# Tile 0's value rows summed by VectorE; other tiles' slots in fours, with one Gelu and one product for their diagonals; convolution taps spread over 40 positions

## What is computed

```python
z = x @ w_in                                  # q, k, v (8 heads x 64), GLU value and gate
att = dilated sliding-window attention        # prompt: over 1024 keys; sample: over a cache
conv = swish(LN(causal depthwise conv, 31 taps))
x1 = LN(ALPHA * x + concat(att, conv) @ w_out)
# PEER: 8 heads; each takes the 16 best of 128 x 128 product keys -> 128 experts a token
act = gelu(einsum('td,tkd->tk', x1, expert_u[e]))      # k = 128 slots
coef = softmax(best scores) * act
y = LN(ALPHA * x1 + einsum('tk,tkd->td', coef, expert_v[e]))
```

## Time and profile before

| | |
|---|---|
| median of 3 runs | 4052.86 us (4046.16 to 4052.99) |
| the profiled execution: its time | 4054.08 us |
| its span | 4052.3 us |
| DMA traffic over the span | 1385.80 MB, 342 GB/s |
| tile 0, first dot to tile 1's first dot | 909.6 us |
| tiles 1 to 6, from first dot to first dot | 2266.1 us together |
| tile 7 / tile 8 and the end | 505.1 us / 172.0 us |

### The profile page before, as it was taken

How to read it: one execution, slowest core, us unless ns; L and a number is a source line. 1 busy time by engine, 2 the same in 40 slices (tenths; PEclk the granted TensorE clock), 3 DMA queues, 4 the chain that set the end, 5 groups by cost and what they waited for, 6 DMA issues and landing times.

```text
span 4052.3 us, 41343 instructions
## 1 busy us (share of the span) xinstructions
PE 2865.7 (71%) x14768; PEld 1255.5 (31%) x14768; DVE 2703.9 (67%) x7412; ACT 682.6 (17%) x1484; POOL 1203.4 (30%) x1092
## 2 busy tenths in 40 slices
PE   6976554778567667666766876687677666779766
PEld 5422221334222313332332333233223332223311
DVE  4233343335586998699679868976997696445965
ACT  1200012210022013102310330132014101121000
POOL 0011111111144433433444344424333442223232
PEclk8987777889788888888888888879878988889989
DMA  9954468577689998998999899979988999999888
GB/s 334 345 202 155 151 225 290 206 277 291 226 328 408 411 366 326 422 413 345 372 419 400 330 395 419 394 290 416 414 355 325 421 408 391 415 417 365 335 329 349
DMA packets 217518, 1385.80 MB, mean 342 GB/s; under 512 B 27416, under 2 KB 38168, under 8 KB 66648
## 3 DMA queue, kind: packets, MB, share of 16 engines
q0 software_dynamic: 156672, 1140.92, 70.6%
q1 hardware_dynamic: 40384, 142.88, 9.8%
q10 hardware_dynamic: 20256, 99.35, 6.4%
HBM read 1369.94 MB, written 80.04 MB: 358 GB/s over the span
## 4 chain that ended last, share of the span: by engine, by line
PE 33%; DMA 29%; DVE 25%; issue 10%; POOL 2%; ACT 1%; DVEq 0%; ACTq 0%; POOLq 0%; SPq 0%
DMA t<-in_expert_uv,t 28%; PE psum L1367 20%; DVE t L1036 8%; PE psum L1214 4%; DVE t L1047 3%; PE psum L1256 2%; PE psum L1234 2%; POOL t L603 2%; DVE t L984 1%; DVE t L982 1%; DVE t L985 1%; DVE t L983 1%; PE psum L1245 1%; DVE t L927 1%; DVE t L981 1%
## 5 line engine op out<-in xcount | busy, mean ns | idle before, releaser
L1367 PE MATMUL psum<-t,t 64*64 64x512 f32 x5696 | 1627.2, 712 | 777.9 <-DVE t L1047 777.6
L603 POOL DMA_INDIRECT t<-in_expert_uv,t x1088 | 1203.2, 1106 | 2819.4 <-PE psum L1367 1403.2
L1036 DVE CUSTOM_DVE_ANT_0 t<-t,t 128x1024 f32<-128x1024 f32 x1088 | 1325.2, 1222 | 1039.0 <-DMA t<-in_expert_uv,t 1031.5
L1367 PEld LDWEIGHTS psum<-t,t 64*64 64x64 f32 x5696 | 415.9, 155 | 1746.1 <-DVE t L1047 983.1
L1363 PE MATMUL psum<-t,t 64*64 64x512 f32 x2496 | 760.4, 738 | 0.0
L754 ACT ACTIVATE t<-t 128x2 f32<-128x2 f32 x544 | 110.6, 203 | 2472.5 <-DVE t L1036 2465.6
L1047 DVE TENSOR_SCALAR t<-t,t,t 128x64 f32<-128x64 f32 x1088 | 294.0, 321 | 68.0 <-ACT t L754 59.1
L1324 PEld LDWEIGHTS psum<-t,t 128*128 128x128 f32 x2304 | 271.7, 197 | 54.0 <-issue 53.9
L1324 PE MATMUL psum<-t,t 128*128 128x128 f32 (+1 forms) x2304 | 281.8, 282 | 0.0
L1214 PE MATMUL psum<-t,t 128*128 128x128 f32 (+2 forms) x768 | 253.8, 489 | 8.2 <-DMA t<-in_xT 7.5
L903 DVE SCALAR_TENSOR_TENSOR t<-t,t,t 128x128 f32<-128x128 f32 x840 | 237.8, 344 | 0.0
(11 more groups left out here) (132 smaller groups left out, 1965.4 us busy)
## 6 DMA issues: line engine op xcount, KB each, us to landing
t<-in_wq_t ACTq DMA_DIRECT2D x63, 1024.0 KB
out<-in_cache_k_win SPq DMA_DIRECT2D x8, 4080.0 KB
out<-in_cache_v_win SPq DMA_DIRECT2D x8, 4080.0 KB
t<-in_w_in_t ACTq DMA_DIRECT2D x44, 512.0 KB, 5.1
t<-in_kc_t SPq DMA_DIRECT2D x8, 2560.0 KB
t<-in_vc_t SPq DMA_DIRECT2D x8, 2560.0 KB, 13.7
t<-in_expert_uv,t POOLq DMA_INDIRECT x1088
t<-in_w_v_t ACTq DMA_DIRECT2D x6, 1024.0 KB, 8.6
```

Of the source, the lines that this page charges most:

```text
L603: pool.indirect_dma_start(ring[:, r, :], None, I["expert_uv"], bass.IndirectOffsetOnAxis(ap=idn[t % 2][:, s:s + 1], axis=0)).then_inc(land ...
L1036: dve.tensor_tensor_reduce(out=ring[:, r, 0:D], in0=x1[t % 2][:, :], in1=ring[:, r, 0:D], scale=1.0, scalar=0.0, op0=ALU.mult, op1=ALU.add ...
L1367: last = pe.matmul(MAIN[t][half][NS * a:NS * a + NS, :], zt[NS * a:NS * a + NS, k % Z_RING, j, :], vv[NS * a:NS * a + NS, :], start=(p == ...
```

## The change

Tile 0's slots no longer go to TensorE. VectorE multiplies a pair's two Gelus with their gates and then adds each slot's v half, scaled by the token's weight, to a sum of 128x1024 in PSUM (`first_values`); it raises `v_done` slot by slot, and `gather` of the slot four later waits for that. In the other tiles four slots make a batch: one Gelu of 128x4, on VectorE one product of 128x4 with the gates and one product of 128x4x64 for the four diagonals, on TensorE the four slots' products one after the other and one step of `pv`. `zt` has two buffers of four. VectorE handles a batch one position after its last slot, behind that position's `dot`; TensorE at the same position. In stage -1 there are 48 slots of tile 0 (49 before), so that their gates are those of three heads. The taps are spread over 40 positions. The steps between attention and routing move: conv LayerNorm to g 10 to 12, both halves of the output projection to g 13 (i = 1 and 3), the LayerNorm of `x1` to g 14 and 15, `queries` and `query_copy` from i = 1 and 2 to i = 3 of their group. The diff, cut to its core:

```diff
 RING, FIRST_RING = 9, 4
-Z_RING = 3
-PAIRS = SLOTS // 2
+Z_RING = 2
+PAIRS, QUADS = SLOTS // 2, SLOTS // 4
...
+TAP_SPAN = 40
...
-EARLY = ROUTE_STEP
-EARLY_GATES = (EARLY * (PH - 1) + TOP - 1) // TOP
+EARLY = 3 * TOP
+EARLY_GATES = EARLY // TOP
...
-AUX_PAIRS = range(8, PAIRS - 4)
+AUX_QUADS = range(3, QUADS - 2)
...
-    early = EARLY * (PH - 1)
     if n < 0:
-        lo, hi = (min(max(q + j - ROUTE_AT - ROUTE_STEP, 0), early) for j in range(2))
+        lo, hi = (min(max(q + j - ROUTE_AT - ROUTE_STEP, 0), EARLY) for j in range(2))
     elif n == 0:
-        lo, hi = (early + (q + j) * (SLOTS - early) // SLOTS for j in range(2))
+        lo, hi = (EARLY + (q + j) * (SLOTS - EARLY) // SLOTS for j in range(2))
...
+def batch(t):
+    return 4 if t else 2
...
+def tap_at(q):
+    return range(q * CK // TAP_SPAN, (q + 1) * CK // TAP_SPAN) if q < TAP_SPAN else range(0)
...
-        zt = small([P, Z_RING, 2, NS])
+        zt = small([P, Z_RING, 4, NS])
...
                 r, use = spot(t, s)
                 if t == 0:
                     if s >= FIRST_RING:
-                        pool.wait_ge(pv, pair(0, s - FIRST_RING) + 1)
+                        pool.wait_ge(v_done, s - FIRST_RING + 1)
                 else:
                     k = (t - 1) * SLOTS + s
                     if k >= RING:
-                        pool.wait_ge(pv, pair(1, k - RING) + 1)
+                        pool.wait_ge(pv, (k - RING) // 4 + 1)
                     elif k < FIRST_RING:
-                        pool.wait_ge(pv, pair(0, SLOTS - FIRST_RING + k) + 1)
+                        pool.wait_ge(v_done, SLOTS - FIRST_RING + k + 1)
                     elif k == FIRST_RING:
...
-            def gelu(t, p):
-                act.wait_ge(a_dot, SLOTS * t + 2 * p + 2)
-                d_ = dots[t % 2][:, 2 * p:2 * p + 2]
+            def gelu(t, c):
+                w = batch(t)
+                act.wait_ge(a_dot, SLOTS * t + w * (c + 1))
+                d_ = dots[t % 2][:, w * c:w * (c + 1)]
                 act.activation(d_, d_, ACT.Gelu).then_inc(a_gelu, 1)
...
-                act.wait_ge(pv, PAIRS * t + AUX_PAIRS.stop)
+                act.wait_ge(pv, quad(t, AUX_QUADS.stop))
...
+                for h in range(PH):
+                    if g == QUERY_AT[h] and i == 3:
+                        query_copy(m, h)
+                        if h == 0:
+                            x1_rows(m)
                 if i != 2:
                     return
-                if g == 9:
+                if g == 11:
                     conv_std(m)
-                if g == 10:
+                if g == 12:
                     conv_swish(m)
                     attended(m)
                     route_loads(m)
-                if g == 13:
+                if g == 14:
                     ln1_std(m)
-                if g == 14:
...
                         score_copy(m, h)
-                    if g == QUERY_AT[h]:
-                        query_copy(m, h)
-                        if h == 0:
-                            x1_rows(m)
...
                                          scalar=0.0, op0=ALU.mult, op1=ALU.add, accum_out=dots[t % 2][:, s:s + 1]).then_inc(a_dot, 1)
-            def weigh(t, p):
-                k = PAIRS * t + p
-                dve.wait_ge(a_gelu, k + 1)
+            def weigh(t, c):
+                k = quad(t, c)
+                d4, g4 = dots[t % 2][:, 4 * c:4 * c + 4], gtn[t % 2][:, 4 * c:4 * c + 4]
+                dve.wait_ge(a_gelu, gelus(t, c) + 1)
+                step(dve.tensor_tensor(d4, d4, g4, ALU.mult))
                 if k >= Z_RING:
                     dve.wait_ge(pv, k - Z_RING + 1)
-                for j in range(2):
-                    s = 2 * p + j
-                    dve.tensor_scalar(zt[:, k % Z_RING, j, :], ident2[:, :], dots[t % 2][:, s:s + 1], gtn[t % 2][:, s:s + 1],
-                                      ALU.mult, ALU.mult).then_inc(zt_ready, 1)
+                dve.tensor_tensor(zt[:, k % Z_RING, :, :], ident2[:, :].unsqueeze(1).broadcast_to([P, 4, NS]),
+                                  d4.unsqueeze(2).broadcast_to([P, 4, NS]), ALU.mult).then_inc(zt_ready, 1)
+            def first_values(c):
+                d2 = dots[0][:, 2 * c:2 * c + 2]
+                dve.wait_ge(a_gelu, gelus(0, c) + 1)
+                step(dve.tensor_tensor(d2, d2, gtn[0][:, 2 * c:2 * c + 2], ALU.mult))
+                for s in (2 * c, 2 * c + 1):
+                    r, _ = spot(0, s)
+                    w_ = dots[0][:, s:s + 1]
+                    if s == 0:
+                        dve.tensor_scalar(first_sum, ring[:, r, D:ROW], w_, None, ALU.mult).then_inc(v_done, 1)
+                    else:
+                        dve.wait_ge(v_done, s)
+                        dve.scalar_tensor_tensor(first_sum, ring[:, r, D:ROW], w_, first_sum, ALU.mult, ALU.add).then_inc(v_done, 1)
             def residual(t):
                 r = rows(t)
-                if t in AUX_TILES:
+                if t == 0:
+                    dve.wait_ge(v_done, SLOTS)
+                elif t in AUX_TILES:
                     dve.wait_ge(aux_in, AUX_TILES.index(t) + 1)
                 else:
-                    dve.wait_ge(pv, PAIRS * t + slots(t) // 2)
+                    dve.wait_ge(pv, quad(t, slots(t) // 4))
                 s_, r_ = stat2[0:r, :], x1[t % 2][0:r, :]
                 for half in range(2):
                     sl = slice(half * 512, half * 512 + 512)
...
                     gates_end(PT, gate_events(PT), range(PH))
             def front(m, g, i):
-                if m and 4 * g + i < CK:
-                    taps(m, 4 * g + i)
+                for k in tap_at(4 * g + i) if m else ():
+                    taps(m, k)
                 if i == 1 and 2 <= g < PH + 2:
                     weights_sum(m, g - 2)
                 if i == 2 and 1 <= g < PH + 1:
                     weights_max(m, g - 1)
-                if g == 9 and i == 2:
+                if g == 11 and i == 0:
                     conv_var(m)
-                if g == 9 and i == 3:
+                if g == 11 and i == 3:
                     conv_norm(m)
-                if g in (12, 13) and i == 2:
-                    ln1_half(m, g - 12)
-                if g == 14 and i == 0:
+                if g == 14 and i in (0, 1):
+                    ln1_half(m, i)
+                if g == 15 and i == 0:
                     ln1_end(m)
                 h, at_ = divmod(4 * g + i - ROUTE_AT, ROUTE_STEP)
...
                 for g in range(GROUPS):
                     for i in range(4):
                         q = 4 * g + i
-                        for t, p in pairs_at(n, q, 2):
-                            weigh(t, p)
                         for s in slots_at(n, q):
                             dot(max(n, 0), s)
+                        for t, c in batches_at(n, q, 1):
+                            if t:
+                                weigh(t, c)
+                            else:
+                                first_values(c)
                         if n >= 1 and q == RESIDUAL_AT:
                             residual(n - 1)
                         if m < PT:
...
                 last.then_inc(a_s, 1)
-            def values_pair(t, p):
-                k = PAIRS * t + p
-                w = slots(t) // 2
-                aux = t in AUX_TILES and p in AUX_PAIRS
-                if p == 0:
+            def values_quad(t, c):
+                k = quad(t, c)
+                w = slots(t) // 4
+                aux = t in AUX_TILES and c in AUX_QUADS
+                if c == 0:
...
-                if aux and p == AUX_PAIRS.start:
+                if aux and c == AUX_QUADS.start:
                     pe.wait_ge(res_done, t)
-                pe.wait_ge(zt_ready, 2 * (k + 1))
-                for half in range(2):
-                    for j in range(2):
-                        r, _ = spot(t, 2 * p + j)
-                        vv = ring[:, r, D + half * 512:D + (half + 1) * 512]
...
+                pe.wait_ge(zt_ready, k + 1)
+                for two in range(2):
+                    for half in range(2):
+                        for j in (2 * two, 2 * two + 1):
+                            r, _ = spot(t, 4 * c + j)
+                            vv = ring[:, r, D + half * 512:D + (half + 1) * 512]
+                            if t == PT:
+                                last = pe.matmul(MAIN[t][half][0:NS, :], zt[:, k % Z_RING, j, :], vv, start=(c == 0 and j == 0), stop=(c == w - 1 and j == 3))
+                            elif aux and j % 2:
+                                for a in range(2):
+                                    last = pe.matmul(AUX[t][half][NS - NS * a:P - NS * a, :], zt[NS * a:NS * a + NS, k % Z_RING, j, :], vv[NS * a:NS * a + NS, :],
+                                                     start=(c == AUX_QUADS.start and j == 1), stop=(c == AUX_QUADS.stop - 1 and j == 3))
+                            else:
+                                for a in range(2):
```

(37 more changed lines are left out.)

## The result

The changed kernel takes 4112.99 us (median of 4 runs, 4107.61 to 4120.43), against 4052.93 for the kernel before on the same chip: ratio 1.0153, 95% interval 1.0134 to 1.0173. It is slower by about 60 us. The forecast was 3760, its range 3700 to 3895. The profiled execution took 4120.43 us with a span of 4118.6, 66.3 more than before.

A forecast was written before the change was run, and what follows sets the result against it. Tile 0 was taken as bound by a ring loop of gathers, dots and TensorE's products, tiles 1 to 6 as near full DMA. Terms -136 - 120 + 0 - 42 - 3 + 7 = -294 us took 4054.1 to 3760, range 3700 to 3895.

The forecast's parts named there:

- Tile 0: First tile: VectorE's sums shorten the loop; slots 0 to 47 save 136 us, slots 48 to 127 save 120 us.
- The sums are dear: Rival, tile 0: VectorE's PSUM writes or a held issue add 1.25 us to 64 pairs, +80 us, 3840 us; chance 0.12.
- Tile 0 gives half: Rival, tile 0: the chain of queries, scores and copies for each head is late next; +128, 3888 us; chance 0.05.
- Tiles 1 to 6: Tiles with four slots a batch: the ring's middle just fits, the ends don't; -7 us a tile, -42 us.
- tile 8: Last tile: eight slots need 20.8 us against 20, +3 us; the last batch ends 3.65 later, +4 us.
- Tile 7: Tile 7 at 3.9 us a slot, its last 32 slots by VectorE: -3 us.
- The ring of nine is short: Rival: batches released late, +1.2 us on 110 loops of eight slots, +130, 3890 us; chance 0.17, no change at all 0.03.
- Slower: Rival: TensorE falls to its low clock between batches, +365 us for seven tiles and a part, 4125 us; chance 0.06.
- Full DMA: Rival, tiles 1 to 6: VectorE's relief closes the transfers' gaps, -78 us further, 3682 us; chance 0.09.

The follow-up runs named there:

- With pairs: The changed kernel, moved steps included, with two slots to a batch in all tiles instead of four: 3743.35 us, ratio 0.9250 to the kernel before.
- Pairs with seven places: The changed kernel with two slots to a batch in all tiles, using seven of the ring's nine places from tile 1 on: 3953.03 us, ratio 0.9762.
- both cures together: The changed kernel, still four to a batch, with release by two slots and tiles 1 to 6's diagonals at the batch's own last position: 3903.49 us, ratio 0.9631.
- Nine, eight and seven places: The changed kernel with two slots to a batch in all tiles, using nine, eight or seven ring places from tile 1 on: 3743.35, 3800.48 and 3953.03 us.

## Why the prediction was wrong

**Tile 0: right, in mechanism and in size.** Forecast 228 and 425 us, measured 231.3 and 421.3. The term without a row, the sum over 128x1024 with PSUM as input and output, was taken at 1.25 us and took 1.29 over 127 instructions. One pair of positions in the changed kernel's timeline:

```profile
282.94 1.23 DVE L1053 CUSTOM_DVE_ANT_0 t<-t,t 128x1024 f32<-128x1024 f32 x1 [2.46 <-DMA t<-in_expert_uv,t]
...
284.28 2.61 DVE L1079 SCALAR_TENSOR_TENSOR psum<-t,t,psum 128x1024 f32<-128x1024 f32 x2
...
285.84 0.94 POOL L618 DMA_INDIRECT t<-in_expert_uv,t  x1 [7.14 <-DVE psum L1079]
287.17 0.94 POOL L618 DMA_INDIRECT t<-in_expert_uv,t  x1 [0.39 <-DVE psum L1079]
```

The gather follows the first sum at once, and the second sum runs beside its issue, as the working had it. That the sum would not hold up the issue, priced at nothing, was right too: of tile 0's 128 issues 60 had a sum and no dot beside them, and they took 0.94 us each, none over 0.95. Issues did become longer, 1.05 us on average in slots 0 to 47 (50.47 / 48) where they were 0.94, but by the dots: the 27 with a dot beside them took 1.44 us, the longest 2.18. The trace before already had this: in its tiles 1 to 6 the 545 issues with a dot beside them took 1.23 us and the other 223 took 0.95. The rule of the Trainium skill (GPSIMD Engine Reference, Key points), that instructions with two SBUF inputs contend with GpSimd, says the same: the dot has two and the sum has one. *The sums are dear* and *Tile 0 gives half* did not happen.

**Tiles 1 to 6: wrong, and with them the sign.** The step that failed reads: "So eight slots (two batches share the ring) need 19.5 us, or 23 us at the tile's first 12 and last 8 slots, against 20 us of transfers. The middle just fits". The loop that the working named, with its places and its order, was the right one; its terms were too small. Means over the turns in the middle of tiles 2 to 6, worked out from the trace of the changed kernel:

| term of the turn, us | in the forecast | measured |
|---|---|---|
| diagonals' end to products | 0.06 | 0.54 |
| products of four slots | 3.9 | 5.24 |
| release to issue | 0.3 | 0.40 |
| issue to the first freed slot's dot | 5.75 | 8.42 |
| first to fourth dot | 7.5 | 8.40 |
| fourth dot to the diagonals' end | 2.0 | 2.3 |
| eight slots | 19.5 | 25.3 |

The largest error is the flight. 5.75 us was read in tile 0, at a DMA share of 0.50; in tiles 1 to 6 the share is 0.87 and the other batch's gathers and the weight loads are under way beside it. Of the 8.42 us, 7.5 passed until the row had landed and 0.9 until its dot. The figure for the loaded stage was to be had: there the trace before has 13.2 us from issue to dot, part of it a landed row's wait for its turn. The second is the products. 3.9 us priced TensorE's steps at the high level of its clock; in the rows above a batch begins at 1.12 and 1.06 us a step after 5.51 us of idle and reaches 0.59 only at its end. The ends of the tiles, where two products run at once, came to 8.67 us where 7.3 was set, in turns of 31.7 us against 23; tile 8 to 8.49, in turns of 24.4 against 20.8: on its eight turns that is 29 us, about the 27 by which tile 8 missed. (Its forecast of +3 should have been +6 by its own 0.8 us a turn, a slip that changes nothing.) Tile 7, priced by VectorE's relief alone, never had its loop worked out: two products at once all through, 542.5 us.

A smaller step fell with it: 12 us a tile off slots 0 to 31 because VectorE has less to do there. That needs VectorE to be what each slot waits for last, and with the ring short it is not. With pairs, where the ring has slack, the same kind of relief and the new places together are worth 40 us in the whole kernel (3782.89 - 3743.35).

**The rivals.** *The ring of nine is short* was the one (chance 0.17), priced at +1.2 us on 110 loops, +130 us, "and up to no change at its end". Against the forecast's own stages it came to +361 (294 in tiles 1 to 6, 40 in tile 7, 27 in tile 8). A turn of six terms, each taken near its best, with a slack under 2 us, had to be priced with all six at their worst as well: the measured 25.3 us against 20 of transfers is 5 us a turn, not 1.2. *Slower*, by TensorE's low level, gave 4125 us, close to what was measured, but not by its mechanism. Its test, a granted clock under 0.75, failed at 0.79, and shifting the time of release alone moved 184 us while that clock moved by 0.02. It may have a part: the products' 1.3 us of the 5.8 by which the turn was too short. The page of the Trainium skill (TensorE: Matmul & The Clock Gate, Part 1), which says that the throttled state is the default and activity releases it, agrees with the rows of a batch, 1.06 us a step first and 0.59 last. How much of the time hangs on it no run separated. *Full DMA* did not come, and not with pairs either: it needed tiles 1 to 6 to take 120 us less than before, and with pairs, at a share of 0.96 and 2.90 us a slot, they took 37 less (2229.3 against 2266.1).

**The tests** named ahead worked: "the share in tiles 1 to 6 under 0.93, with GpSimd waiting for TensorE longer than now" is what the trace shows. Tile 0's did too (first to first dot near 655 us: 652.6; gathers waiting for VectorE's sum).

**What stays open.** Pairs with seven places keep as many gathers under way as the change (3.33 and 3.22) and take 2398.8 us in tiles 1 to 6 against 2518.6. And both cures together keep 4.47 under way, as the kernel before does, and take 2360.9 us against 2266.1. So a batch of four costs more than the places that it holds. The rest may be the burst in which four gathers start, the products' length or the ends of the tiles; that is argued, not shown.

## What to carry to other kernels

Batching saves instructions on one engine and takes places in a ring from another. Before batching, count the places a batch holds and for how long, and write out the turn from release to release; here a turn worked out at 19.5 us against 20 of transfers took 25.3, so a slack of a few per cent is none. Take each duration of the turn from the stage in which it will run, the flight of a transfer at that stage's DMA load, the products at the level at which a batch starts. And where one change has several parts, take the part that stands by itself: here VectorE's sum for tile 0, with pairs and the moved steps, gives 3743 us, 0.925 of the time before.

## What the runs showed of the hardware that was not expected

- VectorE's accumulation with PSUM as input and output over 128x1024 took 1.29 us each time, only 5% more than the 1.22 of a product of that size. GpSimd's issues of gathers beside it took 0.94 us; with a dot (two inputs, both in SBUF) beside them they took 1.44 on average in tile 0, with neither 0.98.
- A gather of 1 MB took 5.75 us from issue to dot at a DMA share of 0.50, and 8.4 us to the first dot of a freed slot in the middle of tiles 2 to 6, where the share was 0.87; over all 1088 gathers of the change the median from issue to landing was 9.5 us.
- Nine, eight and seven places of 1 MB gave 2229, 2284 and 2399 us for 768 slots: the rate fell from 387 to 361 GB/s, with 5.15, 4.22 and 3.33 gathers under way.
